# Attention as one pipeline over 36 slots, with transposes made by the DMA engines

## The reference

```
h  = LN_in(x)
z  = h @ W_in -> [retention q,k,v,gate | dilated-attention q,k,v]
m  = concat(swish(gate) * HeadNorm(Retention(q,k,v)), DilatedAttn(q,k,v)) @ W_out
h1 = LN1(alpha * h + m)
f  = ConvFFN(h1)
e  = sigmoid(h1 @ W_pg) * (p[i] @ W_pp)
h  = LN2(alpha * h1 + f + e)
```

## Time and profile before

| | |
|---|---|
| median of 3 runs | 1692.08 us (1691.21 to 1696.86) |
| the profiled execution, its own time | 1693.98 us |
| its span, first to last instruction | 1692.2 us |
| mean granted clock of TensorE | 0.952 |
| attention stage, from its first matmul to the first of the next stage | 333.4 to 653.6 us |
| TensorE, VectorE, ScalarE, GpSimd busy | 90%, 50%, 27%, 12% of the span |

### The profile page before, as it was taken

One profiled execution on the slowest core, in us unless ns is written; L12 is line 12 of the kernel. 1 busy time (PEld: TensorE's weight loads), 2 busy tenths in 40 slices (PEclk: granted clock), 3 DMA queues, 4 the chain that ended last, 5 costly groups with the idle time before them and its releaser, 6 DMA issues. The chain is left out here.

```text
span 1692.2 us, 26128 instructions
## 1 busy us (share of the span) xinstructions
PE 1528.6 (90%) x9284; PEld 870.6 (51%) x9284; DVE 851.0 (50%) x1820; ACT 457.6 (27%) x742; POOL 210.0 (12%) x132
## 2 busy tenths in 40 slices
PE   1699999799999998389799899999999999999994
PEld 1355555456565654135344466645665466645641
DVE  6566766536465675656512145513553245513457
ACT  2321121125353452012311134401442034401310
POOL 4311010010101011512200001100111001100125
PEclk9999999798998998589999999999999999999997
DMA  7001001110201024641100322201221012201002
GB/s 218 26 26 51 27 24 39 36 49 17 63 10 59 26 76 131 208 153 47 53 10 3 98 82 74 75 0 37 74 74 37 25 50 74 74 0 38 13 18 88
DMA packets 107456, 96.63 MB, mean 57 GB/s; under 512 B 6551, under 2 KB 91367, under 8 KB 107127
## 3 DMA queue, kind: packets, MB, share of 16 engines
q1 hardware_dynamic: 107391, 95.78, 18.8%
HBM read 85.79 MB, written 10.15 MB: 57 GB/s over the span
## 5 line engine op out<-in xcount | busy, mean ns | idle before, releaser
L1532 PE MATMUL PS<-all_HT,all_WS 128*128 128x344 f16 x3168 | 465.0, 310 | 6.6 <-POOLq L74 4.9
L1532 PEld LDWEIGHTS PS<-all_HT,all_WS 128*128 128x128 f16 x3168 | 310.6, 98 | 161.6 <-issue 8.5
L1542 PE MATMUL PS<-all_WS,ffn_HG 128*128 128x512 f16 x704 | 211.0, 379 | 3.9 <-POOL ffn_HG L1643 1.9
L442 PE MATMUL PS<-all_WS,all_HT 128*128 (+3 forms) x864 | 195.1, 383 | 3.8 <-POOLq L74 3.8
L740 PE MATMUL PS<-all_WS,all_HT 128*128 (+3 forms) x864 | 148.3, 329 | 5.5 <-POOLq L74 3.4
L1617 ACT ACTIVATE ffn_C<-PS,all_CW,all_CWS 128x1032 f32<-128x1032 f32 x44 | 53.1, 1206 | 362.6 <-PE PS L1532 362.6
L1643 POOL TENSOR_TENSOR ffn_HG<-ffn_PRD,ffn_HG 128x1032 f32 (+1 forms) x22 | 47.2, 2147 | 748.8 <-ACT ffn_HG L1629 748.8
L442 PEld LDWEIGHTS PS<-all_WS,all_HT 128*128 128x128 f16 (+1 forms) x864 | 83.9, 98 | 101.9 <-issue 4.5
L1542 PE MATMUL PS<-ffn_WD,ffn_HG 128*128 128x512 f16 x352 | 133.4, 379 | 0.0
L1542 PEld LDWEIGHTS PS<-all_WS,ffn_HG 128*128 (+1 forms) x704 | 68.8, 98 | 88.8 <-issue 6.7
L740 PEld LDWEIGHTS PS<-all_WS,all_HT 128*128 128x128 f16 (+1 forms) x864 | 82.8, 97 | 60.6 <-issue 8.3
(11 more groups left out here) (207 smaller groups left out, 1899.9 us busy)
## 6 DMA issues: line engine op xcount, KB each, us to landing
ffn_SU<-in_w_up SPq DMA_DIRECT2D x42, 512.0 KB, 4.9
ffn_SD<-in_w_down SPq DMA_DIRECT2D x22, 512.0 KB, 3.5
all_STG<-in_w_in SPq DMA_DIRECT2D x32, 256.0 KB, 3.2
all_STG<-in_w_in SPq DMA_DIRECT2D x32, 192.0 KB, 2.6
samples_KC<-in_cache_k_win SPq DMA_DIRECT2D x24, 256.0 KB, 3.7
all_HRES<-in_x_prompt SPq DMA_DIRECT2D x8, 512.0 KB, 5.0
out<-attention_QKV SPq DMA_DIRECT2D x8, 512.0 KB
all_STG<-in_w_out SPq DMA_DIRECT2D x8, 512.0 KB, 3.5
```

Source lines behind the costliest of these rows:

```text
L442: mm = nc.tensor.matmul(Z(s)[:n], HT[:, a, k, s * P:s * P + n], WS[:, slot, b, k, :], start=(k == 0 and (a, b) == (0, 0)), stop=(k == KD - ...
L1532: mm = nc.tensor.matmul(U(x)[:, third], UW[:, u, a, k, x * P:(x + 1) * P], HT[:, b, k, third * T3:(third + 1) * T3], start=(k == 0 and (a, ...
L1542: mm = nc.tensor.matmul(DB[u][:rows, half], HG[:, a, l, ds(t * P, rows)], WD[b][:, l, half * 512:(half + 1) * 512], start=(l == 0 and (a, ...
```

## The change

Attention becomes one loop over 36 slots g = 9p + s. In each slot TensorE projects slot g, scores the tile of slot g-2 (`LS`) for both heads of the pair, and makes the value products of slot g-5 (`LP`). There are no separate phases, and all is written out without a hardware loop.

- A step x = 2i + h is one head of tile i. VectorE runs mask(x), inverse sum(x-1), low half(x-2) in turn, and ScalarE exponential(x), high half(x-1). So three steps are in work at once (`PR` has three buffers).
- Probabilities are normalised before they are split: the reciprocal of the sum, times 1024, goes into the high half as a scale (an Identity activation) and into the low half (a scalar_tensor_tensor). Both halves lie beside each other in `P16`, in fp16 and in SBUF.
- The transposes of the probabilities and of q and k are DMA transposes, issued by SyncE: one for each step x, of up to 16 blocks of 128x128, and one of four blocks for q and k of each tile. TensorE makes no transposes in the stage.
- GpSimd splits q and k (`QK16`) and v for every tile.
- The score matmuls alternate between the heads, in partitions 0 to 63 and 64 to 127. In the value products v gives the 64 columns of weights and the transposed probabilities stream through; the heads write to partitions 0 to 63 and 64 to 127 of `OB`. So the result comes out transposed and `ATT` is not needed. Every fourth tile ScalarE and VectorE write four tiles of it to `MT`.
- The rotation reads `QKV` in SBUF, after ScalarE's copy. `QKV` has four buffers, and keys and values are stored for each tile.
- `QKT` and V16 have two buffers, for two pairs. Four buffers hold `P16` and `PRT`.

```diff
+            LS, LP = 2, 5
...
+                    def turn_qk(g):
+                        i, p, q = tile_of(g)
+                        if i is not None:
+                            sp.wait_ge(qk_lo, BASE + i + 1)
+                            sp.wait_ge(qk_turned[i % 2], BASE + 16 * (i // 2))
+                            if p >= 2:
+                                sp.wait_ge(scored, BASE + NT * (p - 1))
+                            sp.dma_start_transpose(QKT[:, p % 2, q], QK16[:, i % 2].rearrange("p a n -> p (a n)")).then_inc(qk_turned[i % 2], 16)
...
+                    def turn_p(g):
+                        for x in range(max(0, reach(g - 1, 2)), reach(g, 2)):
+                            i, q = x // 2, x // 2 % NT
+                            sp.wait_ge(p_lo, BASE + x + 1)
+                            if i >= 2:
+                                sp.wait_ge(o_ready, BASE + i - 1)
+                            sp.dma_start_transpose(PRT[:, x % 4, 0:2 * (q + 1)],
+                                                   P16[:, x % 4, 0:2 * (q + 1) * P]).then_inc(p_turned[x % 4], 16)
...
+                        turn_qk(g - 1)
+                        store(g - 1)
+                        if g < NG:
+                            for c in ({0: (0, 1), 5: (2,), 6: (3,), 7: (4,), 8: (5,)} if p == HP - 1 else {0: (0, 1), 2: (2,), 4: (3,)}).get(s, ()):
+                                load_w(p, c)
...
+                        turn_p(g)
...
+                    def score(g):
+                        i, p, q = tile_of(g)
+                        if i is None:
+                            return
+                        pe.wait_ge(qk_turned[i % 2], BASE + 16 * (i // 2 + 1))
+                        if i >= 1:
+                            pe.wait_ge(qk_turned[(i - 1) % 2], BASE + 16 * ((i - 1) // 2 + 1))
+                        pe.wait_ge(masked, BASE + 2 * i)
...
+                    def values(g):
...
+                            pe.wait_ge(p_turned[x % 4], BASE + 16 * (x // 4 + 1))
+                        pe.wait_ge(v_lo, BASE + i + 1)
...
+                                    mm = nc.tensor.matmul(OB[h * E:(h + 1) * E, q // 4, (q % 4) * P:(q % 4 + 1) * P],
+                                                          V16[p % 2][:, b, kb, h * E:(h + 1) * E],
+                                                          PRT[:, (2 * i + h) % 4, a * (q + 1) + kb],
...
+                    for g in range(NG + LP):
+                        if g < NG:
+                            project(g)
+                        score(g - LS)
+                        values(g - LP)
...
+                    def high(x):
+                        w = (x // 2 % NT + 1) * P
+                        act.wait_ge(rcp_ready, BASE + x + 1)
+                        if x >= 4:
+                            act.wait_ge(p_turned[x % 4], BASE + 16 * (x // 4))
+                        nc.scalar.activation(P16[:, x % 4, 0:w], PR[:, x % 3, 0:w], ACT.Identity,
+                                             scale=RCP[:, x % 4:x % 4 + 1]).then_inc(p_hi, 1)
...
+                        for x in (2 * i, 2 * i + 1):
+                            exponential(x)
+                            if x > reach(g - 1, 1):
+                                high(x - 1)
...
+                    for g in range(NG + LP + 2):
+                        soften(g)
+                        split(g)
+                        out(g - LP - 1)
+                        copy(g)
...
+                        for x in (2 * i, 2 * i + 1):
+                            mask(x)
+                            if x > max(0, reach(g - 1, 1)):
+                                invert(x - 1)
+                            if x > 1 + max(0, reach(g - 1, 2)):
+                                low(x - 2)
...
+                    for g in range(NG + LP + 2):
+                        soften(g)
+                        split(g)
+                        out(g - LP - 1)
+                        rotate(g)
```

More of the change, by code:

```diff
@@ new lines, in reach, with stored @@
+            def reach(g, lag):
+                i, p, q = tile_of(g - LS - 1)
+                if i is not None:
+                    return 2 * i + 2 - lag
+                return 2 * sum(tile_of(j)[0] is not None for j in range(g - LS))
+            def stored(g):
+                return sum(48 if i % (NT + 1) == NT else 32 for i in range(g % 4, g, 4))
+            (tab_in, z_ready, copied, halves, rotated, qk_hi, qk_lo, v_hi, v_lo, scored, masked, neg_ready, exp_ready, rcp_ready,
+             p_hi, p_lo, o_ready, mhi, mlo, w_free, whi, scaled) = sems(
+                "tab_in z_ready copied halves rotated qk_hi qk_lo v_hi v_lo scored masked neg_ready exp_ready rcp_ready "
+                    "p_hi p_lo o_ready mhi mlo w_free whi scaled")
@@ L671, in _ @@
+                    for u in range(4):
+                        sp.wait_ge(out_st[u], BASE + stored(NG + u))
                     clear_before(sp)
@@ new lines, in out @@
+                    def out(g):
+                        i, p, q = tile_of(g)
+                        if i is not None and q % 4 == 3:
+                            act.wait_ge(o_ready, BASE + i + 1)
+                            nc.scalar.activation(MT[:, 0, HP + p, (q - 3) * P:(q + 1) * P], OB[:, q // 4], ACT.Copy,
+                                                 scale=S_ACT / S_P).then_inc(mhi, 1)
+                    for g in range(NG + LP + 2):
[3 more added lines that the diff above has]
+                        copy(g)
@@ new lines, in soften @@
+                    def soften(g):
+                        i, p, q = tile_of(g - LS - 1)
+                        if i is None:
+                            for x in range(max(0, reach(g - 1, 1)), reach(g, 1)):
+                                invert(x)
+                            for x in range(max(0, reach(g - 1, 2)), reach(g, 2)):
+                                low(x)
+                            return
+                        for x in (2 * i, 2 * i + 1):
[4 more added lines that the diff above has]
+                                low(x - 2)
@@ new lines, in out @@
+                    def out(g):
+                        i, p, q = tile_of(g)
+                        if i is not None and q % 4 == 3:
+                            dve.wait_ge(mhi, BASE + i // 4 + 1)
+                            w = MT[:, :, HP + p, (q - 3) * P:(q + 1) * P]
+                            nc.vector.scalar_tensor_tensor(w[:, 1], OB[:, q // 4], S_ACT / S_P, w[:, 0], ALU.mult,
+                                                           ALU.subtract).then_inc(mlo, 1)
+                    for g in range(NG + LP + 2):
+                        soften(g)
+                        split(g)
+                        out(g - LP - 1)
+                        rotate(g)
```

440 lines of the change are left out of this document (184 added, 256 removed).

## The result

The changed kernel took 1648.4 us (median of 4 runs, 1645.8 to 1650.8) where the one before took 1694.5 on the same chip: a ratio of 0.973, with an interval of 0.972 to 0.975. So it is faster, by 46 us. Forecast was 1617, 75.5 us less than before; the range held the time, and the likeliest case's own band, up to 1650, just held it too. The profiled execution took 1648.5 us where the same sum gave 1618.5. What has to be explained is why these 30 us of the gain did not come.

The account below looks back on a forecast made before the run. TensorE, busy nearly nine tenths of the span, was taken as the bound. Four pairs of 57.5 us, less 11.3, plus a 26 us tail gave a 244.7 us stage against 320.2, 75.5 less: 1617 us, range 1598 to 1705.

Parts of the forecast that it names:

- the likeliest case: Whole kernel: the forecast including unoverlapped matmul halves and GpSimd holding VectorE up, 1598 to 1650 us; chance 0.60.
- A: Rival in scores and values: matmul halves don't overlap, 62.6 us a pair, 1637 us; inside the forecast's 0.60.
- E: Rival on VectorE: GpSimd holds it up, 1 us in three slots a pair, 12 us, 1629; inside the 0.60.
- B: Rival: DMA transposes set the pace, stage still below today's; 67 us a pair, 1655 us, up to 1687; chance 0.15.
- C: Rival: DMA transposes set the pace and make the kernel slower; at 70 GB/s 91 us a pair, 1751 us; chance 0.20.
- Scores and values: TensorE's matmuls per key block, two heads partly overlapping: 0.24 us scores, 0.25 us values; 54.5 us a pair with projection.
- VectorE and ScalarE's loop in a pair: Mask-to-next-mask loop crossing both engines: 2.5 to 8.3 us a slot, 49.3 a pair; larger of it and TensorE, 57.5.
- I take this as hidden at a cost inside the 57.5: DMA transposes of probabilities and q/k: 50 us a pair at 141 GB/s, hidden within the pair's 57.5 us.
- The tail, 26 us: After the last projection: tiles 6 and 7 softened beside four weight splits, then transposes, values, output; 26 us unhidden.
- The first pair: Start of the stage: nothing softened or multiplied in slots 0 to 3, so 11.3 us less than a pair's 57.5.
- Clock near 1.0: TensorE in the stage never idles long, so clock near 1.0; contained in 4.1 us per projection and 0.054 per 128 columns.
- D: Rival on ScalarE: Identity among exponentials forces 32 table loads of 1.28 us a pair, 1747 us; chance 0.02.

Follow-up runs that it names:

- two blocks a transpose: Changed kernel, every DMA transpose of probabilities moving two 128x128 blocks (64 KB) instead of up to sixteen (512 KB): 1633.5 us, ratio 0.9639.
- the order turned: Changed kernel, SyncE issuing tile 7's probability transposes before the q/k transpose, stores and loads in slot 2: 1635.4 us, ratio 0.9648.
- the three edits together: Changed kernel with tile 7's transposes first in slot 2, that slot's weight load in slot 4, one output weight split a slot in the tail: 1632.0 us.

## Why the prediction came out as it did

*Direction and mechanism: right; that the likeliest band held the time: luck.* No transpose is left on TensorE, the alternation of the two phases is gone, and 47 us came off the stage. But the band reached to 1650 because A (1637) and E (12 us more) lay in it. A did not occur and E is at most 5.4 us in the two pairs tried; what carried the time to 1648 were waits for transposes, for which the sum had nothing, and a longer tail. Two of the signs that I had named for being wrong or for B and C came true: slots over 9 us (13.5, 12.4, and 9.8 in the last pair), and values that wait for transposes.

*Scores and values: mis-sized, without effect.* I took 0.24 and 0.25 us per key block. Adding the groups of one pair (0.34 to 1.47 us for scores, 0.36 to 1.53 for values at full clock) gives 7.2 and 7.6 us for 36 blocks, 0.20 and 0.21. The halves run together. Rival A, that they don't, is refuted. TensorE's pair is then 51.7 us, not 54.5, and the pairs gained nothing from it.

The Trainium skill ("TensorE: Matmul & The Clock Gate", part 3) had said that matmuls in different row or column tiles run at once. The trace agrees: 12 score matmuls in 1.47 us, where twice the 1.30 of the earlier trace rows would be 2.6.

*VectorE and ScalarE's loop in a pair: right in sum, in part by luck.* All slots but slot 3 make 50.5 us for 50.9. Single slots are off by up to 1.9 us and cancel (slot 1 shorter, slots 2 and 8 longer), and in slots 1 and 2 of the second pair 1.2 and 1.9 us are waits for transposes, which the sum did not have; with two blocks a transpose slot 1 takes 5.1 us, where the loop had been given 8.3.

*"I take this as hidden at a cost inside the 57.5": the step that failed.* It had two parts. The rate was about right: in the 5 us from 408 to 413 the DMA engines were full at 164 GB/s (the stores beside the transposes included), where I had 141 for pieces of 256 bytes, and tile 7 took about the 9 us that I gave it from issue to landing. But I looked at the queue in one direction only, q/k behind probabilities, and called that safe. What happened is the other one: the probabilities of the widest tile stand behind q/k, stores and loads of the next slot. And I counted the slack from the wrong end. "Values five slots behind" is counted from the projection; tile 7's last low half ends only in slot 2, and its values are due in slot 3, 6.5 us later, while the chain (2.4 us of queue, 5.2 of issuing, 3.6 to landing) takes 11.1. In the second pair slot 3 is 6.9 us over the forecast: 4.65 of wait and 2.9 of slow clock, less 0.6 by which TensorE's own work is below the forecast. The wait can be taken away from either end: the order turned brings the values 4.3 us sooner, an eighth of the widest tile's data 5.1. With the order turned the second pair takes 58.4 us, and 0.9 us remain of the 6.5.

The Trainium skill ("DMA: Bandwidth & Descriptors", latency and other measured facts) gives 261 GB/s for DMA transposes with a non-contiguous middle dimension. Here full engines moved 164; the measurement decides.

*The tail, 26 us: mis-sized by 8.7 with the slot before it.* Forecast for both were 32.8, measured 41.5. Most comes before the last low half: 4.7 us in the loops of tiles 6 and 7 and 2.1 before tile 6's first mask. I had the two splits of a slot at 1.2 us each; but VectorE's half of a split needs ScalarE's, so at the end of each loop 1.9 us of waiting come before the 2.4 that VectorE takes. Slow clock on the last values (2.77 us for 1.53) and the longer landing are most of the rest. The kernel with two blocks shows that the size of the transposes is 2.8 us of it; spreading the splits took 2.3 us out of the loops and 0.9 out of the tail. No run removed all of the splits, so their full share stays open.

*The first pair* is 2.8 us too long. No run was made to tell why, but the trace shows where: the first three projections took 14.4 us instead of 12.2, at a granted clock of 0.82 (0.50 in the first 5 us, behind a wait of 2.9 us), and slot 8 took 8.0 for 6.8, with 1.90 us of waiting for masks.

*Clock near 1.0: wrong in slot 3 and the tail.* 0.95 in the first three pairs, 0.93 in the last and 0.73 in the tail; the slow groups stand behind waits. In the pairs and the tail it comes with the two steps above, and is not a step of its own.

*Rivals.* B and C, transposes as the pace, are refuted as such: waits for transposes exist in slots 1 to 3, but the other slots keep a pace that transposes do not set, and one eighth of the widest tile's data brings little more in the sum (1633.5 us) than a better order (1635.4). D is refuted: the stage has one table load in all. E is right in kind; its size, 2.4 and 3.0 us in two pairs beside 12 us guessed for four, rests on one execution and holds the earlier q/k transposes too, and it lies mostly in other slots than named. GpSimd takes 0.87 us for the first split of 256 columns and about 2.9 us a tile, where I had 0.69 and 2.2.

The Trainium skill ("SBUF — State Buffer", SBUF: two separate sides) says that a VectorE operation with two SBUF inputs and GpSimd share a pair of ports, which one of them locks for a whole instruction. That the low half and GpSimd's operation get longer beside each other, and that the mask does not, agrees. That one stands still for the other's whole instruction is not shown: a low half grew by 0.22 us beside GpSimd operations of 0.85 us and more.

So of 28.6 us, some 17 are the waits around slot 3 and, in the last pair, slot 2 (6.5, 6.4 and 4.2 us in three pairs, of which the order alone gives back 13.7 and the three edits together 13.1), 8.7 the tail, and 2.8 the first pair. What remains in the version with three edits, 15.7 us of the stage above the forecast, is mainly the tail (7.1) and the first pair (4.5).

## What to carry to other kernels

When one queue issues everything, write down for each heavy item what stands ahead of it, not only what stands behind it; the widest tile decides, and its slack must be counted from the moment at which its last input is ready. To tell order from size, look at when the transfers are issued and when their user starts, not at the length of the slot in which it waits: that length also grows when the slots before it shrink. A mean rate that fits says only that the transfers can be hidden, not that they are. And a tail has no other work to cover a split that crosses two engines: add the halves one after the other there.

## What the hardware showed that I had not expected

- Issuing a DMA transpose takes SyncE 1.17 to 3.26 us, and it lands 2.3 to 6.3 us after its issue; cut to 64 KB, still 1.17 to 2.36 and 2.3 to 4.9.
- Score matmuls of two heads in the two row halves overlap even when one head's three follow the other's (12 in 1.48 us); value matmuls in the two column halves took 1.03 us for 30 when they alternated, and 1.67 in turn.
- A busy GpSimd slows VectorE where VectorE works in SBUF alone (1.50 against 1.28 us at 1024 columns, one execution each), and not where it reads PSUM (1.22 both times).
- A wait can cost TensorE more than its length: after 4.65 us of it, 48 matmuls took 2.77 us; after 1.97 us, 1.53. Its length does not settle it: in another kernel, behind a wait of 1.99 us, they took 2.35.
